# Mixture-of-experts stage: rounds of two experts' items against items served one at a time, rows moved by indirect transfers

## The reference, cut to what matters

```python
def hier_moe(h, wr_g, br_g, wr_e, br_e, w_gate, w_up, w_down):
    ...
    expert_id = (g_sel * EXPERTS_PER_GROUP + e_sel).reshape(-1)     # 2 of 32 experts for each of 512 tokens
    ...
    def expert_block(args):
        xb, e = args
        return (jax.nn.silu(xb @ w_gate[e]) * (xb @ w_up[e])) @ w_down[e]   # 1024x512, 1024x512, 512x1024
    ...
    y_rows = y_rows * row_gate[:, None]
    out = jnp.zeros((n_tok + 1, d)).at[row_token].add(y_rows)[:n_tok]

for i in range(DEPTH):        # DEPTH = 2
    ...
    x = x + g2[:, None, :] * hier_moe(h, ...)
return rmsnorm_2(x, final_norm_g)
```

## Time and profile before

| | us |
|---|---|
| median of 3 runs | 4006.45 |
| lowest to highest | 4001.98 to 4007.94 |
| profiled execution (span) | 4008.1 |

### The profile page before, as it was taken

The page is one execution under the profiler, slowest core; times in us unless marked ns, Lnnn a source line. Parts: engine busy times, 40 slices in busy tenths (PEclk is TensorE's granted clock), DMA queues, the critical chain, the costliest instruction groups (busy, mean ns, idle before and its releaser), DMA issues. The chain is left out here.

```text
span 4008.1 us, 38008 instructions
## 1 busy us (share of the span) xinstructions
PE 3480.4 (87%) x13936; PEld 1752.2 (44%) x13937; DVE 1688.1 (42%) x3091; ACT 701.3 (17%) x1412; POOL 196.3 (5%) x263
## 2 busy tenths in 40 slices
PE   8998999888899999889889977778699978788775
PEld 4454434885444444378634432223243344422222
DVE  3235556775232555567548420000238766200002
ACT  1132204000112330310010100000122243100001
POOL 0001010001000001000000000000100130000000
PEclk9999999999999999899889989999889989799998
DMA  3115452004121226200143099999533421799996
GB/s 105 68 48 209 143 169 60 1 1 144 47 89 32 68 83 208 55 11 1 59 175 122 0 396 429 428 428 399 202 105 121 110 73 62 310 429 419 429 428 283
DMA packets 208086, 696.40 MB, mean 174 GB/s; under 512 B 22248, under 2 KB 105704, under 8 KB 182608
## 3 DMA queue, kind: packets, MB, share of 16 engines
q1 hardware_dynamic: 178576, 589.56, 38.4%
q0 software_dynamic: 29376, 105.05, 7.2%
HBM read 636.28 MB, written 58.28 MB: 173 GB/s over the span
## 5 line engine op out<-in xcount | busy, mean ns | idle before, releaser
L345 PE MATMUL bank<-fm,w 128*128 128x512 f32 (+1 forms) x912 | 397.3, 596 | 11.4 <-DMA w<-in_ab_w_in 6.3
L2796 PE MATMUL bank<-experts_wu,experts_hs 128*64 128x512 f32 x1120 | 275.8, 650 | 75.0 <-DMA experts_wu<-in_moe_w_up 75.0
L2796 PE MATMUL bank<-experts_wg,experts_hs 128*64 128x512 f32 x1120 | 272.2, 642 | 60.1 <-DMA experts_wg<-in_moe_w_gate 45.6
L345 PE MATMUL bank<-w,fm 128*128 128x512 f32 (+2 forms) x768 | 315.5, 567 | 6.5 <-DMA w<-in_w_in 6.5
L2861 DVE TENSOR_TENSOR fm<-bank,fm 128x512 f32<-128x512 f32 x35 | 37.0, 1056 | 638.9 <-PE bank L2796 638.9
L2796 PE MATMUL bank<-experts_wd,fm 128*64 128x512 f32 x1120 | 256.4, 611 | 45.4 <-issue 24.0
L345 PEld LDWEIGHTS bank<-fm,w 128*128 128x128 f32 (+1 forms) x912 | 172.4, 190 | 234.1 <-issue 221.0
L726 PE MATMUL bank<-fm,side_w 128*128 128x512 f32 x512 | 252.4, 619 | 6.9 <-DMA side_w<-in_w_in 5.4
L345 PEld LDWEIGHTS bank<-w,fm 128*128 128x128 f32 x768 | 142.2, 195 | 179.2 <-issue 153.8
L2796 PEld LDWEIGHTS bank<-experts_wu,experts_hs 128*64 128x64 f32 x1120 | 85.9, 148 | 263.2 <-issue 166.1
L2796 PEld LDWEIGHTS bank<-experts_wg,experts_hs 128*64 128x64 f32 x1120 | 94.6, 147 | 233.6 <-issue 230.5
(11 more groups left out here) (484 smaller groups left out, 4875.5 us busy)
## 6 DMA issues: line engine op xcount, KB each, us to landing
experts_wg<-in_moe_w_gate SPq DMA_DIRECT2D x64, 2048.0 KB, 19.5
experts_wu<-in_moe_w_up SPq DMA_DIRECT2D x64, 2048.0 KB
experts_wd<-in_moe_w_down SPq DMA_DIRECT2D x64, 2048.0 KB
ada_w<-in_ada_w POOLq DMA_DIRECT2D x96, 512.0 KB, 4.9
w<-in_w_in SPq DMA_DIRECT2D x40, 512.0 KB, 3.9
expert_rows<-fm POOLq DMA_DIRECT2D x35, 512.0 KB, 10.3
fm<-expert_rows SPq DMA_DIRECT2D x33, 512.0 KB, 21.6
w<-in_w_in SPq DMA_DIRECT2D x16, 1024.0 KB, 7.2
```

Of the source, the lines that this page charges most:

```text
L345: ins = pe.matmul(bank, lhsT, rhs, start=(n == 0), stop=(n == len(todo) - 1))
L2796: ins = pe.matmul(bank[rows, :], lhs[:, k, rows], weights[:, s, k, cols], start=(k == 0), stop=(k == chunks - 1))
```

## The change

- A round becomes an item of one expert. Experts are served in their order, each to its end; expert e uses the weight buffers of its parity. SP's loads are fixed in the program: for each expert it waits for `weights_free` of that parity, which PE raises once, after the last item of the expert before the previous one, and then issues gate, up and down together.
- Within an item, gate and up stand side by side in the halves of the array (16 products), and so do the two halves of the columns of down (8 products).
- The 64 rows of an item are fetched as 128 half rows of 2 KB by one indirect DMA from POOL out of `token_rows`, which holds the tokens in their own order and is stored with 4 plain DMAs by the stage before (`keep`). The result y (128 x 512) is written by one indirect DMA from POOL to `made_rows`, in the order of the pairs. Both indirect DMAs are preceded by a POOL copy of the item's column of indices. Indices of empty slots are out of bounds.
- POOL's loop is: fetch the rows of item p+1, copy the indices, wait for y of item p, write it, wait until it has landed, free y. PE turns the rows of item p+1 between gate/up and down of item p.
- `plan` makes the tables of indices (one product over 8 pairs of one-hot tables) in place of the tables by round. The product gather of the first rows, the spread to `expert_rows` and its clearing go. `moe_residual` reads the results by plain DMAs from SP.

```diff
-        if cleared_rows is not None:
-            ...
-                for n in range(cleared_rows.shape[0] // P):
-                    pool.dma_start(cleared_rows[n * P:(n + 1) * P, :], zero[:, :]).then_inc(*wiped.inc(16))
...
+    def keep(self, sp, h):
+        for t in range(TILES):
+            sp.wait_ge(*self.norm.normed.at(t + 1))
+            sp.dma_start(self.chip.token_rows[t * P:(t + 1) * P, :], h[:, t, :]).then_inc(*self.chip.tokens_kept.inc(16))
...
     @st.block.sync
     def _(sp):
...
-        with sp.Fori(2, n) as p:
-            seats = first_two(p)
-            sp.wait_ge(*gathered.at(p))
-            load_rows(p + 1)
-            load("moe_w_down", wd, down_done, down_loaded, p, seats)
+        for e in range(EXPERTS):
+            s, before = e % 2, e // 2
+            ...
+            if before:
+                sp.wait_ge(*weights_free[s].at(before))
+            load("moe_w_gate", wg, gate_loaded)
+            load("moe_w_up", wu, up_loaded)
+            load("moe_w_down", wd, down_loaded)
 
     @st.block.gpsimd
     def _(pool):
-        with pool.Fori(0, rounds_of(pool)) as p:
-            pool.wait_ge(*yready.at(p + 1))
-            pool.dma_start(rows[bass.ds(p * P, P), :], y[:, :]).then_inc(*ystored.inc(16))
-            pool.wait_ge(*ystored.at(16 * p + 16))
-            pool.sem_inc(yfree.sem, 1)
+        def fetch(p, picked, number):
+            pool.tensor_copy(now_from[:, :], at_from[:, bass.ds(p, 1)]).then_inc(*picked.inc())
+            pool.wait_ge(*placed.at(1))
+            pool.wait_ge(*picked.at(number))
+            pool.indirect_dma_start(out=xs[:, :], out_offset=None, in_=token_halves,
+                                    in_offset=bass.IndirectOffsetOnAxis(ap=now_from[:, 0:1], axis=0),
+                                    bounds_check=2 * SEQ - 1, oob_is_err=False).then_inc(*rows_loaded.inc(16))
+        ...
+        fetch(0, first_picked, 1)
+        with pool.Fori(0, items_of(pool)) as p:
+            pool.wait_ge(*rows_turned.at(p + 1))
+            fetch(p + 1, picked_from, p + 1)
+            pool.tensor_copy(now_to[:, :], at_to[:, bass.ds(p, 1)]).then_inc(*picked_to.inc())
+            pool.wait_ge(*placed.at(1))
+            pool.wait_ge(*picked_to.at(p + 1))
+            pool.wait_ge(*y_ready.at(p + 1))
+            pool.indirect_dma_start(out=made_halves, out_offset=bass.IndirectOffsetOnAxis(ap=now_to[:, 0:1], axis=0), in_=y[:, :],
+                                    in_offset=None, bounds_check=4 * SEQ + 1, oob_is_err=False).then_inc(*y_stored.inc(16))
+            pool.wait_ge(*y_stored.at(16 * p + 16))
+            pool.sem_inc(y_free.sem, 1)
 
     @st.block.tensor
     def _(pe):
+        def item(j, p, s):
+            pe.wait_ge(*filled.at(p + 1))
+            pe.wait_ge(*gate_loaded[s].at(16 * j + 16))
+            pe.wait_ge(*up_loaded[s].at(16 * j + 16))
             for k in range(DC):
+                rows = hs[:, k % 4, k // 4, :]
+                for half, w in ((slice(0, SLOTS), wg), (upper, wu)):
+                    ins = pe.matmul(B[0][half, :], rows, w[:, s, k, :], start=(k == 0), stop=(k == DC - 1))
+            ins.then_inc(*first_done.inc())
+
+            turn(p + 1).then_inc(*rows_turned.inc())
 
             pe.wait_ge(*hidden.at(p + 1))
             for f in range(FC):
-                ins = pe.transpose(B[2][:, f * P:(f + 1) * P], hid[:, f * P:(f + 1) * P], chip.ident)
+                ins = pe.transpose(B[2][:, f * P:(f + 1) * P], both[:, f * P:(f + 1) * P], chip.ident)
             ins.then_inc(*hturned.inc())
             pe.wait_ge(*hmoved.at(p + 1))
-            pe.wait_ge(*down_loaded.at(landed))
-            ...
+            pe.wait_ge(*down_loaded[s].at(16 * j + 16))
+            for f in range(FC):
+                for d in range(2):
+                    ins = pe.matmul(B[4][d * SLOTS:(d + 1) * SLOTS, :], hidT[:, f, :], wd[:, s, f, d * BANK:(d + 1) * BANK],
+                                    start=(f == 0), stop=(f == FC - 1))
             ins.then_inc(*down_done.inc())
+        with pe.Fori(0, EXPERTS // 2) as j:
+            for s in range(2):
+                ...
+                with pe.Fori(first, end) as p:
+                    item(j, p, s)
+                pe.transpose(B[5][:, 0:P], chip.ident, chip.ident).then_inc(*weights_free[s].inc())
```

More of the change, by code:

```diff
@@ L2463, in _ @@
             routed.load(sp, io, 1)
+            routed.keep(sp, h)
         @st.block.tensor
@@ L2703, in _ @@
-        link(dve.tensor_tensor(t3[0:1, 0:ROUNDS, 0], end, start, ALU.subtract))
-        link(dve.tensor_tensor_scan(landed, chip.ones[0:1, 0:ROUNDS], t3[0:1, 0:ROUNDS, 0], 0.0, ALU.mult, ALU.add))
-        link(dve.tensor_scalar(landed, landed, 16.0, None, ALU.mult))
-        dve.tensor_copy(counts[:, :], row[:, :]).then_inc(*counted.inc())
-def item_experts(chip, st, i, io, fm, counts, counted, gate_row, hs, first_filled, rows, rows_written, weights, weights_loaded):
+        link(dve.tensor_reduce(block[:, :], past[:, :, :], AX.X, ALU.add))
@@ L2712, in item_experts @@
+        link(dve.tensor_scalar(where[:, :, :], where[:, :, :], 2.0, chip.half, ALU.mult, ALU.add))
+        dve.tensor_copy(at_from[:, :], where[:, 0, :])
+        dve.tensor_copy(at_to[:, :], where[:, 1, :]).then_inc(*placed.inc())
+def item_experts(chip, st, i, io, fm, counts, counted, at_from, at_to, placed, gate_half, gated, hs, weights, loaded):
     B = chip.bank
     wg, wu, wd = weights
-    xs, y = part(fm, 0, D), part(fm, D, D)
-    act_out, hid = part(fm, 2 * D, D_EXP), part(fm, 2 * D + D_EXP, D_EXP)
@@ L2910, in experts, with _ @@
-                item_experts(chip, st, i, io, fm, counts, counted, mod[:, 5, :], hs, first_filled, made, written.at(written.total),
-                             weights, weights_loaded)
+                loaded = [[st.count(f"{n}{s}", fresh=True) for s in range(2)] for n in ("gate_loaded", "up_loaded", "down_loaded")]
+                @st.block.scalar
+                def _(act):
+                    for half in range(2):
+                        rows = slice(half * SLOTS, (half + 1) * SLOTS)
+                        act.activation(gate_half[rows, :], mod[rows, 5, half * BANK:(half + 1) * BANK], ACT.Copy).then_inc(*gated.inc())
@@ L2935, in _ @@
             def _(sp):
+                for t, n in order:
+                    at = n * TILES + t
+                    sp.dma_start(rows[:, at, :], chip.made_rows[at * P:(at + 1) * P, :]).then_inc(*fetched[at].inc(16))
                 for c in used:
```

313 lines of the change are left out of this document (104 added, 209 removed).

## The result

| | before | after |
|---|---|---|
| median | 4007.19 us (4001.98 to 4016.57, 4 runs) | 4688.81 us (4684.79 to 4696.43, 4 runs) |
| ratio to before | 1 | 1.1708, 95% interval 1.1686 to 1.173 |
| profiled execution (span) | 4008.1 us | 4694.6 us, clock 0.87 |

A forecast was written before the change was run, and what follows sets the result against it. Weight traffic bound the expert stages before; a chain through POOL would bound them after. Stages 1713 - 1043.6, plus 12 for the start, minus 3 for `moe_residual`, give +678: 4685 us, range 4400 to 4940.

The forecast's parts named there:

- 66 rings: Expert stages: per-item chain from down through scatter, landing, gather and turn to down; 10.7 us plus both transfers, 26.1 us.
- 6 rings without: Expert stages, items without a weight load: undisturbed transfers, 10.7 + 3.7 + 4.4 = 18.8 us each.
- X: POOL's scatter of y beside weight loads, empty slots mostly making no packets: 8.2 us, bounds 6.6 to 10.7.
- (3): POOL between scatter landing and gather issue: wake, raise y_free, branch, index copy, semaphore; 1.2 us.
- F: POOL's gather of the next rows, slowed by weights for its first 6 us: 7.2 us, bounds 5.8 to 9.
- The mechanism: Expert stages: POOL fetches next rows only after y lands, so this chain sets an item's period, 26.1 us against 15.3 by bytes.
- The start: Before each layer's first gate product: index tables and row fetch make gate start 6 us later, 12 for both layers.
- the clearing: Attention stage: removing POOL's clearing of 32 x 512 KB, far from the bound, was costed at nothing.
- the picture of turns: Row transfers beside weights: the delay is 0.82 us for each packet's turn on a DMA engine.
- moe_residual: In that stage eight indirect fetches become plain ones from SP: 3 us off for both layers together.
- weights_free: SP's weight loads: raising it only at an expert's end costs nothing, since weights issued one period earlier have landed.
- The rule of the Trainium skill: POOL transfers at 2.0 us plus bytes over 436 GB/s: ring 15.9 us, change costing about 50 us; not followed.

The follow-up runs named there:

- the ring cut: Changed kernel, with POOL fetching the rows of item p+2 once item p+1 is turned, before writing y of item p: 4000.33 us, ratio to before 0.999.
- half of it cut: Changed kernel, with POOL issuing the gather of item p+2 right after the scatter of item p, without waiting for its landing: 4318.63 us.
- the filler: Changed kernel with 13 useless 128x512 products between gate/up and the turn, keeping PE busy during its wait: 4617.3 us.
- the fetch of 8 KB: Changed kernel, with the gather replaced by a plain POOL transfer of 16 columns (128 rows of 64 B) at the same place: 4523.65 us.
- chained_before: Kernel before, with rows of round p+1 fetched by POOL behind the landing of y of round p-1, by plain DMA instead of SP: 4192.25 us, ratio 1.0473.
- the last experiment: Changed kernel with rows fetched two items ahead, plus weight loads issued as soon as their buffer has been read: 3977.3 us, ratio to before 0.9935.

## Why the prediction was right, point by point

The sum was 1713 us for the stages; 1731.8 were measured. Its parts, for the 66 rings, by medians of the 60 loaded ones:

| | predicted | measured |
|---|---|---|
| 60 rings with a load | 26.1 each, 1566 | 26.86 (mean), 1612 |
| 6 rings without | 18.8 each, 113 | 14.07 (mean), 84 |
| the first items | 34 | 36 |
| (1) down to scatter | 1.4 | 1.6 |
| (2) X, scatter | 8.2 | 8.0 |
| (3) landing to gather | 1.2 | 1.6 |
| (4) F, gather | 7.2 | 7.9 to the turn |
| (5) turn to down | 3.0 | 2.4 |
| (6) down | 5.1 | 5.4 (4.2 to 5.8) |

*The mechanism* was right, and the runs show it: with the ring cut and all else kept, the 680 us are gone; with half of it cut, half are; with the filler the clock's part goes.

*Step X* was right in size and wrong in its working. I had reasoned that empty slots make no packets. They do: every indirect transfer has 80 packets, whether it carries 2 pairs or 61. The DMA view of a scatter with 2 pairs (2619.9 to 2628 us), and of one with many (2994.97 to 3004.6):

```profile
q0 software_dynamic: 80, 0.01, 0.8%
...
made_rows<-fm,now_to POOLq DMA_INDIRECT x1, 7.4
```

```profile
q0 software_dynamic: 80, 0.25, 6.4%
...
made_rows<-fm,now_to POOLq DMA_INDIRECT x1, 9.0
```

The bytes are not what sets these two 1.6 us apart: the median is 7.8 us for the 9 loaded scatters under 30 KB and 8.2 for the 8 over 200 KB, and single ones lie anywhere from 7.2 to 9.3. 80 packets are 5 for each of 16 engines; with my 0.82 for each, 2.9 + 0.4 + 4.1 would have been 7.4, close too. The experiments show that this is chance: 3 us of the delay are fixed, ahead of the first packet, and only the rest goes by turns. That X came within 0.2 us was luck. A good number from a wrong picture would fail on the next size: for the fetch of 8 KB the picture of turns gives 2.0 + 2 x 0.82 = 3.6 us, and 5.9 were measured. (That run's expectation of 5.3 to 5.9 us was near only because I took it to make as many packets as the transfer of 256 KB.)

*F* I had let off lightly because the weights would end at about 17 us of the ring. They land 18 to 19 us after their issue, since both transfers and the start of the loads take their share, so the gather gets no free stretch. That is +0.7 us, and step (3) another 0.4. The range of 5.8 to 9 held it.

*The rings without a load* were mis-sized by 4.7 us each. I had taken 3.7 for the undisturbed scatter, for which the prediction gives no working (its own figures make 2.9 + 0.4 = 3.3), 4.4 for the undisturbed gather, the time from the first of eight fetches to the sum on DVE, and PE at the lower clock. In fact:

```profile
3159.05 1.03 POOL L2738 DMA_INDIRECT made_rows<-fm,now_to  x1 [8.32 <-DVE fm L2811]
...
3163.39 1.05 POOL L2723 DMA_INDIRECT fm<-token_rows,now_from  x1 [0.83 <-POOL now_from L2720]
...
3166.21 0.66 PE L2749 MATMUL bank<-consts,fm 128*128 128x128 f32 x4 [1.92 <-DMA fm<-token_rows,now_from]
...
3167.83 3.65 PE L2772 MATMUL bank<-experts_wd,fm 128*64 128x512 f32 x16 [0.52 <-ACT fm L2798]
```

The scatter takes 2.8 us, the gather 2.8 to the turn, PE waits only 1.9 us, and turn and down run at the higher clock. The two go together: after a wait of 1.9 us the turn ran at the higher clock, after 11.6 to 11.9 it did not. This error (-29 us) and the one on the loaded rings (+46) stand against each other, which is luck as well.

*The start* and the clearing hide each other. Gate starts at 2337.86 in the first layer, only 0.3 later than the earlier trace rows, but the way from the last step of the routing (L2595 before, L2592 after) to the first gate product is 26.1 us against 19.9, and in the second layer 25.6 against 21.0: 6.3 and 4.6 longer, near the 6 each that I gave. What brings the first layer forward is the clearing of `expert_rows`, which I had costed at nothing because POOL issues it while PE works. The attention stage that held it takes 120.6 us from its first product with the decay on DVE (L887) to the first product of `ada_sums` behind it (L1941), and 111.9 after; the ten traces of other kernels without the clearing have 111.0 to 112.1, and `chained_before`, which keeps it, has 120.5. So the clearing cost 8.7 us, and that term of the prediction was wrong; it looked at POOL and PE, and not at the DMA engines, which the clearing filled (205 GB/s over the stage against 69 after). Which transfer waited behind it was not traced. `moe_residual` erred the other way: I took 3 us off for both layers, and from the last store to the end of the program it takes 4.0 us more (37.4 against 33.4), in the first layer 2.0 more to the first sum. What is left, some 6 us, is in attention stages that differ by more than that from trace to trace. Outside the expert stages I had forecast +9 and got +2.1, and that it is so near the truth is a sum of errors.

*`weights_free`* at the end of the expert costs nothing behind this ring, as I said: PE's waits in the profile after are for the fetch of rows, and the weights land a period before they are used. It would have been the next thing, and the last experiment prices it at some 20 us.

*The rule of the Trainium skill* ("DMA: Bandwidth & Descriptors", "Anatomy of one DMA"), 2.0 us and the bytes over 436 GB/s, holds for the transfers of the rings without a load (2.8 measured, 2.6 by the rule) and for none beside one (7.9). A ring of 15.9 us by the rule against 26.9 measured: the loaded row of before was the right one to follow.

## What to carry to other kernels

When a change puts two transfers in line between one product and the next, add up the whole ring with durations of transfers under the load that will be there, and with the products behind the wait at the lower clock; then compare it with the time that bytes or products set. A ring of small steps is cut more cheaply than it is sped up: here one more item of lead for the fetch gave 680 us, while a smaller fetch, shorter weight packets, single loads or a PE at the higher clock gave 70 to 200 us each. A step that costs nothing behind a long ring should be priced again once the ring is gone.

## What the hardware showed that I had not expected

- An indirect transfer makes all its packets, also for indices out of bounds: 80 packets for 2 pairs, 80 for many. The bytes fall (0.01 MB against 0.25), the time hardly does: median 7.8 us beside weights for scatters under 30 KB, 8.2 for those over 200 KB.
- Beside weight loads even a transfer of 8 KB takes 5.9 us against 2.0 alone; with short weight packets 5.3. About 3 us of that go by neither the transfer's size, nor the size of the weights' packets, nor whether one or three loads are queued. They pass before the transfer's first packet starts (3.7 to 4.5 us after the issue, against 1.2 to 1.6 alone). What they are was not found.
- Clearing 16.8 MB with 32 plain DMAs from POOL in an attention stage made that stage 8.7 us longer (120.6 against 111.9), though it was cheap for POOL (17.1 us). The DMA engines moved some 400 to 420 GB/s for 40 us while it ran, in a stage that moves 69 GB/s on average without it.
- Plain and indirect fetches of the same 256 KB take the same time in flight (8.0 and 7.9 us from issue to the turn).
